# Last expert's second layer and its combination split by 256 columns, layer-norm sums taken in halves, and uneven first input pieces, in a hybrid encoder layer

## The chip, the cores and the metric

The kernel runs on one core of one Trainium2 chip. Its time is the device time of one execution, in microseconds (us). Three runs of the kernel before gave 1277.27, 1277.75 and 1278.08 us, median 1277.75. TensorE (PE) does the matrix products, VectorE (DVE) and ScalarE (ACT) the elementwise work; SyncE (SP) and ScalarE issue the transfers (DMA) discussed here.

## The reference

One layer of a streaming encoder over 256 tokens of width 1024, in float32: a combined input projection, four sequence mixers (gated recurrence, latent attention, a diagonal state-space model, a gated linear recurrence), a gated merge, a layer norm, and then a mixture of experts with a second layer norm. Cut to what this change touches:

```python
proj = x @ w_in                                # first: x and the first 256 columns of w_in
...
top_val, top_idx = lax.top_k(logits, TOP_K)    # 4 of 32 experts a token
top_w = jax.nn.softmax(top_val, axis=-1)
...
y = clamped_swiglu(xb @ w1[e] + b1[e]) @ w2[e] + b2[e]   # each expert, its tokens
out = zeros(n, d).at[slot_token].add(y * slot_w[:, None])
...
x = layer_norm(ALPHA * h + out, ln2_w, ln2_b)  # mean, variance, scale, shift over 1024
```

## The kernel before

Every weight is read once from device memory, 459 MB in all, nearly all of it the experts' (4 MB for w1 and w2 units of 2 MB each, six units an expert). SP issues the weight transfers in one fixed order, each as soon as the place that it writes is free (the semaphore `expert_chunk_used` counts units that PE has used). PE takes them in the same order. Every wait and every order is written out by hand, engine by engine; nothing is scheduled by a planner.

**The start.** PE first multiplies a matrix of ones by itself, eight times (`warm_up(8)`, L937). The activations `xT` (8 rows of 128 x 256, 1 MB) come by ACT's queue and the first chunk of `w_in` (the same size) by SP's, each in four pieces of two eighths; both queues add to the semaphore `first_in[i]` of piece i. PE waits for piece i and does its eight products (L947), 32 instructions of the trace in all, since each float32 product shows as two. Behind the pieces SP issues seven whole chunks of 1 MB at once (rows of 8 KB a partition, where the pieces have 2 KB). ACT issues the small transfer `vec` when piece 2 has landed and the next ones when the last piece has (L582 to L589).

**The end.** The last two experts, 30 and 31, use 64 rows each (CAP, the tokens given to one expert in the main pass). Expert 31's w2 comes as four transfers of 1 MB (L522): first 512 output columns (dh = 0) of both halves of the hidden width, then the others. `last_columns` (L1407) multiplies 64 rows by 512 columns. Its products for even and odd k go to the two halves of the array's columns, so that two run side by side, and the result lies in rows 0 to 63 and 64 to 127 of bank dh as two partial sums. ACT copies each bank (`last_out`, L844). `first_combine` (L1428) multiplies expert 30's result by the token weights, 64 rows deep, and leaves the sum open; `last_combine` (L1436) adds expert 31's, 128 rows deep, since the weights are there twice and so add the partial sums. DVE then adds each of the four 128 x 512 results to `y_acc` and takes the row sum in the same instruction (L2270), and does the layer norm: centre and scale by `ln2_w` (L2277), reciprocal root (L2279), scale and shift by `ln2_b` (L2282), for tokens 0 to 127 (half 0) and then 128 to 255 (half 1). ACT takes the sums of squares between (L869 to L871). SP sends half 0 out whole (L536) and half 1 in two pieces (L539). `ln2_w` and `ln2_b`, 512 KB each as broadcast to 128 partitions, are issued behind the w2 pieces (L524, L525). If an expert has more than 64 tokens, a loop after the main pass does the rest; in the profiled execution DVE passes it by (L2238).

## Time and profile before

| what | value |
|---|---|
| median of three runs | 1277.75 us |
| the profiled execution | 1277.71 us |
| its span (first to last instruction) | 1275.9 us |
| mean granted TensorE clock | 0.996 |
| PE busy | 1236.8 us, 97% |
| DVE / ACT busy | 457.0 / 219.1 us |
| transfers | 458.63 MB, mean 359 GB/s |

The execution is 1.81 us longer than its span, which lies outside what the trace shows. From about 415 us on, the slices of the profile show 414 to 435 GB/s until the end; before that the rate is mostly 127 to 270. PE's busy time counts matmuls that wait in the pipeline, so 97% does not mean that it could do no more.

### The profile page before, as it was taken

What the parts mean: (1) busy time and instruction counts of PE and PEld (TensorE: products, weight loads), DVE (VectorE), ACT (ScalarE), POOL (GpSimd) and SP (SyncE); (2) the same over time, 40 slices, a digit from 0 to 9 for tenths busy, and PEclk for the clock granted to TensorE, in tenths of its full rate; (3) what the DMA queues carried; (4) which work ended last, traced back from release to release, by engine and by line L of the source; (5) the groups of instructions that cost most, each with busy time, mean ns of one, the idle gap of its engine ahead of it and who ended that gap; (6) DMA issues with size and microseconds to landing.
All of it is one profiled execution on the core that took longest, in us unless ns stands there. A gap on an engine that the chain in (4) does not pass through costs nothing.

```text
span 1275.9 us, 14764 instructions
## 1 busy us (share of the span) xinstructions
PE 1236.8 (97%) x6060; PEld 635.1 (50%) x6060; DVE 457.0 (36%) x915; ACT 219.1 (17%) x428; POOL 2.9 (0%) x14
## 2 busy tenths in 40 slices
PE   9999999999999999999999999999999999899996
PEld 8888888888863343333433333333323333333432
DVE  5999926636344512122121213212121313122123
ACT  1722124230041110101101011110101010110102
POOL 0000000000000000000000000000000000000000
PEclk9999999999999999999999999999999999999998
DMA  9533334346979999999999999999999999999996
GB/s 379 206 133 137 127 134 168 127 165 244 423 269 414 428 433 425 429 432 432 431 432 432 429 435 429 434 430 432 430 432 432 431 433 428 431 430 427 426 425 259
DMA packets 31486, 458.63 MB, mean 359 GB/s; under 512 B 4913, under 2 KB 5169, under 8 KB 9426
## 3 DMA queue, kind: packets, MB, share of 16 engines
q1 hardware_dynamic: 27728, 453.00, 84.5%
q10 hardware_dynamic: 3714, 5.00, 1.2%
q8 instruction: 33, 0.54, 0.2%
q14 instruction: 11, 0.09, 0.0%
HBM read 456.94 MB, written 1.05 MB: 359 GB/s over the span
## 4 chain that ended last, share of the span: by engine, by line
PE 73%; DMA 16%; DVE 7%; issue 1%; ACT 1%; DVEq 0%; SPq 0%; POOL 0%; POOLq 0%
PE banks L1345 20%; DMA store<-in_moe_w 16%; PE banks L916 15%; PE banks L1381 14%; PE banks L1353 4%; PE banks L930 4%; PE banks L1172 2%; PE banks L1197 2%; DVE store L2136 2%; PE banks L1452 2%; PE banks L1261 2%; PE banks L1363 1%; DVE store L2133 1%; DVE store L2135 1%; DVE store L2130 1%
## 5 line engine op out<-in xcount | busy, mean ns | idle before, releaser
L1345 PE MATMUL banks<-store 128*64 128x512 f32 x1536 | 344.0, 597 | 15.6 <-DMA store<-in_moe_w 15.3
L1345 PEld LDWEIGHTS banks<-store 128*64 128x64 f32 x1536 | 109.3, 137 | 232.2 <-issue 208.0
L1381 PE MATMUL banks<-store 128*64 128x512 f32 x952 | 210.8, 595 | 0.0
L916 PE MATMUL banks<-store 128*128 128x256 f32 x896 | 197.0, 380 | 0.0
L916 PEld LDWEIGHTS banks<-store 128*128 128x128 f32 x896 | 169.3, 190 | 26.4 <-issue 3.8
L2130 DVE TENSOR_SCALAR store<-banks 128x512 f32<-128x512 f32 x32 | 22.1, 692 | 429.3 <-PE banks L1353 429.3
L1381 PEld LDWEIGHTS banks<-store 128*64 128x64 f32 x952 | 65.8, 137 | 142.8 <-issue 120.1
L1353 PE MATMUL banks<-store 128*64 128x512 f32 x512 | 116.8, 598 | 0.4 <-DMA store<-in_moe_w 0.4
L2144 DVE COPY store<-banks 64x512 f32<-64x512 f32 x30 | 20.8, 694 | 202.9 <-PE banks L1381 202.9
L795 ACT ACTIVATE store<-store 128x512 f32<-128x512 f32 x28 | 17.6, 630 | 431.3 <-DVE store L2130 431.3
L1353 PEld LDWEIGHTS banks<-store 128*64 128x64 f32 x512 | 34.3, 136 | 70.1 <-issue 67.7
L1261 PEld LDWEIGHTS banks<-store 128*128 128x128 f32 x480 | 56.9, 191 | 23.5 <-issue 23.5
L1261 PE MATMUL banks<-store 128*128 128x128 f32 x480 | 63.7, 281 | 0.0
L1452 PE MATMUL banks<-store 128*128 128x512 f32 x120 | 63.5, 631 | 0.0
L930 PE MATMUL banks<-store 128*128 128x256 f32 x256 | 56.2, 379 | 0.1
L930 PEld LDWEIGHTS banks<-store 128*128 128x128 f32 x256 | 48.3, 190 | 7.3 <-issue 1.0
L784 ACT ACTIVATE store<-banks,ln_cols 128x128 f32<-128x128 f32 x128 | 46.4, 475 | 3.1 <-PE banks L1261 1.9
L803 ACT ACTIVATE store<-banks 64x512 f32<-64x512 f32 x28 | 16.5, 589 | 169.5 <-PE banks L1381 169.5
L1452 PEld LDWEIGHTS banks<-store 128*128 128x128 f32 x120 | 19.1, 188 | 43.7 <-issue 43.7
L2154 DVE TENSOR_TENSOR store<-store,banks 128x512 f32<-128x512 f32 x60 | 37.4, 681 | 1.0 <-PE banks L1472 0.9
L1197 PE MATMUL banks<-store 32*64 32x512 f32 x256 | 34.8, 613 | 0.0
L2136 DVE SCALAR_TENSOR_TENSOR store<-store 128x512 f32<-128x512 f32 x32 | 33.6, 1050 | 1.1
(386 smaller groups left out, 827.1 us busy)
## 6 DMA issues: line engine op xcount, KB each, us to landing
store<-in_moe_w SPq DMA_DIRECT2D x72, 4096.0 KB, 30.3
store<-in_moe_w SPq DMA_DIRECT2D x36, 2048.0 KB, 15.1
store<-in_w_in SPq DMA_DIRECT2D x30, 1024.0 KB, 4.9
store<-in_moe_w SPq DMA_DIRECT2D x18, 1024.0 KB, 9.2
store<-in_w_branch SPq DMA_DIRECT2D x8, 1024.0 KB, 4.9
store<-in_w_out SPq DMA_DIRECT2D x4, 1024.0 KB, 6.7
store<-in_w_last SPq DMA_DIRECT2D x4, 1024.0 KB, 34.8
store<-in_w_first SPq DMA_DIRECT2D x4, 256.0 KB, 4.3
```

The source lines that it names most:

```text
L784: ins = nc.scalar.activation(xg[:, k, :], src, ACT.Identity, scale=ln1_cols[:, 2 * KD + k:2 * KD + k + 1], bias=ln1_cols[:, 3 * KD + k:3 * ...
L916: last = mm(b[:, j * SEQ:(j + 1) * SEQ], w[:, k, j * P:j * P + P], xT[:, k, :], start=k == 0, stop=k == KD - 1)
L930: last = mm(bank[3 + u % 2][:, i * SEQ:(i + 1) * SEQ], w[:, k, c * P:(c + 1) * P], yT[:, br, k, :], start=k == 0, stop=k == 3)
L1197: mm(bank[into[i]][64 * ct:64 * ct + 64, :], esel[r:r + NE, :], b1_all[r:r + NE, :], start=True, stop=False, tile_position=(r, 64 * ct))
L1261: last = mm(bank[2 + k // 4][:, (k % 4) * P:(k % 4) * P + cols], h_tok[:, half, k * P:k * P + P], sel[:, half, 0:cols], start=half == 0, s ...
L1345: last = mm(bank[into[i]][64 * ct:64 * ct + 64, :], xg[:, 2 * c + kk, col:col + CAP], w[:, kk, i * FF + ct * 512:i * FF + ct * 512 + 512], ...
L1353: last = mm(bank[into[i]][64 * ct:64 * ct + 64, :], xg[:, 2 * c + kk, col:col + CAP], w[:, kk, i * FF + ct * 512:i * FF + ct * 512 + 512], ...
L1381: last = mm(bank[4][64 * dh:64 * dh + 64, :], actT[:, j, 64 * fh:64 * fh + 64], w[j][:, 512 * dh:512 * dh + 512], start=(fh, j) == (0, 0), ...
L1452: mm(bank[COMB_BANK[i]][:, :], wselT[0:rows_, half, :], y_pair[0:rows_, 512 * dh:512 * dh + 512], start=True, stop=True).then_inc(S["comb_ ...
L2130: V.tensor_scalar(g1, bank[from_[0]][:, :], LIMIT, None, ALU.min).then_inc(S["gmin_ready"], 1)
L2136: V.scalar_tensor_tensor(g1.rearrange("p (j q) -> p q j", j=4), g2.rearrange("p (q j) -> p q j", j=4), 1.0, g3.rearrange("p (q j) -> p q j ...
L2154: ins = V.tensor_tensor(dst, dst, bank[COMB_BANK[i]][:, :], ALU.add)
```

## The change

Five things change.

1. The input pieces are one, two, two and three eighths. The first chunk and `xT` are stored so that each piece is contiguous in device memory. The warm-up has six products.
2. Expert 31's w2 is laid out by quarters of columns: a transfer holds columns 256 i to 256 i + 255 of both 512-column groups. `last_columns` multiplies by 256 columns and puts the two groups (dh) on the two halves of the array's columns, with one full sum each and no partial ones. The last 1 MB is two transfers of 512 KB, the first of which uses `first_in[0]` again, and SP waits for it before it issues `ln2_w` and `ln2_b`.
3. ACT's copies are 128 x 256. `last_combine` is 64 rows deep, eight products of 256 columns, and writes other places (`LAST_BANK`) than `first_combine`, which is now closed by itself.
4. DVE adds expert 30's four results by themselves (four TENSOR_TENSOR), before the test for the extra loop. PE's last combination waits for these.
5. DVE's four sums with a row sum are now half 0 (i = 0, 1), then half 1. The wait for `ln2_in` comes behind them. Then both L2277 instructions, and after them the scale, shift and output of half 0 and half 1.

```diff
+LAST_BANK = ((6, 2), (4, 0))
+FIRST_ROWS = ((0, 1), (1, 3), (3, 5), (5, KD))
...
             for i in range(pieces):
-                ks = slice(KD // pieces * i, KD // pieces * (i + 1))
-                sp.dma_start(first[:, ks, :], src[i]).then_inc(first_in[i], 16)
+                ks = FIRST[i]
+                src = A["w_first"][0, P * CW * ks.start:P * CW * ks.stop].rearrange("(p k n) -> p k n", p=P, n=CW)
+                sp.dma_start(first[:, ks, :], src).then_inc(first_in[i], 16)
...
-            for dh in range(2):
+            for i in range(2):
                 for c in range(NW1, NU):
-                    sp.dma_start(tail_at(NE - 1, c)[:, SLOT * dh:SLOT * dh + SLOT], A["w2_last"][c - NW1, dh]).then_inc(late_landed[late(NE - 1, c, dh)], 16)
+                    if (i, c) == (1, NU - 1):
+                        for part, signal in ((slice(0, D), first_in[0]), (slice(D, SLOT), late_landed[late(NE - 1, c, i)])):
+                            sp.dma_start(tail_at(NE - 1, c)[:, SLOT:][:, part], A["w2_last"][c - NW1, i][:, part]).then_inc(signal, 16)
+                    else:
+                        sp.dma_start(tail_at(NE - 1, c)[:, SLOT * i:SLOT * i + SLOT], A["w2_last"][c - NW1, i]).then_inc(late_landed[late(NE - 1, c, i)], 16)
             sp.wait_ge(S["expert_chunk_used"], LAST - 3)
+            sp.wait_ge(first_in[0], 48)
...
-            warm_up(8)
+            warm_up(6)
...
-                for k in range(4):
-                    r = 64 * (k % 2)
-                    last = mm(bank[dh][r:r + 64, :], actT_last[:, k, 64 * fh:64 * fh + 64], w[:, k, :],
-                              start=(fh, k // 2) == (0, 0), stop=(fh, k // 2) == (1, 1))
+                for k in range(4):
...
+                    for dh in range(2):
+                        last = mm(bank[i][64 * dh:64 * dh + 64, 0:CW], actT_last[:, k, 64 * fh:64 * fh + 64], w[:, k, CW * dh:CW * dh + CW],
+                                  start=(fh, k) == (0, 0), stop=(fh, k) == (1, 3))
...
-            def last_combine(dh):
-
-                pe.wait_ge(S["ypair_lo"] if dh == 0 else S["ypair_hi"], NE)
+            def last_combine(i):
+
+                pe.wait_ge(S["ypair_hi"] if i else S["ypair_lo"], NE)
+                pe.wait_ge(S["comb_used"], NPAIR * 4 + 4)
                 for half in range(2):
-                    mm(bank[COMB_BANK[2 * half + dh]][:, :], wselT_last[1][:, half, :], y_columns[dh], start=False, stop=True).then_inc(S["comb_psum"], 1)
+                    for dh in range(2):
+                        r = 64 * dh
+                        last = mm(bank[LAST_BANK[i][half] + dh][:, 0:CW], wselT_last[1][r:r + 64, half, :], y_last[1][r:r + 64, CW * i:CW * i + CW],
+                                  start=True, stop=True, tile_position=(r, 0))
+                    last.then_inc(S["comb_psum"], 1)
...
+            for half in range(2):
+                for i in range(2):
+                    piece, added = last_pieces(i, half)
+                    dve.wait_ge(S["comb_psum"], (NPAIR + 1) * 4 + 2 * i + half + 1)
+                    ins = V.scalar_tensor_tensor(piece, added, 1.0, piece, ALU.mult, ALU.add,
+                                                 accum_out=small[:, 316 + 2 * half + i:317 + 2 * half + i])
+                link(ins)
...
             dve.wait_ge(S["ln2_in"], 32)
...
```

PE at the start of the program, before. Line 937 is the warm-up, 947 the first chunk, each row a run of equal products:

```order
L937 MATMUL banks<-ones 128x128 [waits ones_ready]
L937 MATMUL banks<-ones 128x128 x7
L947 MATMUL banks<-store 128x256 [waits first_in0]
L947 MATMUL banks<-store 128x256 x3
L947 MATMUL banks<-store 128x256 [waits first_in1]
...
L947 MATMUL banks<-store 128x256 [waits first_in3]
L947 MATMUL banks<-store 128x256 x3
```

PE at the same place after the change (lines 944 and 954 are the same two):

```order
L944 MATMUL banks<-ones 128x128 [waits ones_ready]
L944 MATMUL banks<-ones 128x128 x5
L954 MATMUL banks<-store 128x256 [waits first_in0]
L954 MATMUL banks<-store 128x256
L954 MATMUL banks<-store 128x256 [waits first_in1]
...
L954 MATMUL banks<-store 128x256 [waits first_in3]
L954 MATMUL banks<-store 128x256 x5
```

Two products of the first piece have gone to the last, and two warm-up products are gone.

DVE at the end, before. 2270 adds and sums, 2277 centres, 2279 is the reciprocal, 2282 scales and shifts:

```order
L2264 MEMSET small 128x1 [waits ln2_in]
L2270 SCALAR_TENSOR_TENSOR store,small<-banks,store 128x512 [waits comb_psum,f_chain] x3
L2273 TENSOR_SCALAR small<-small 128x1 [waits f_chain]
L2270 SCALAR_TENSOR_TENSOR store,small<-banks,store 128x512 [waits comb_psum]
L2273 TENSOR_SCALAR small<-small 128x1 [waits f_chain]
L2277 SCALAR_TENSOR_TENSOR store<-store,small 128x1024 [waits sum_ready]
L2279 RECIPROCAL small<-small 128x1 [waits rs_ready,f_chain]
L2282 SCALAR_TENSOR_TENSOR store<-store,small 128x1024 [waits f_chain]
L2277 SCALAR_TENSOR_TENSOR store<-store,small 128x1024 [waits sum_ready]
```

DVE there after the change (2294, 2302, 2306 and 2309 are these four):

```order
L2288 MEMSET small 128x1
L2294 SCALAR_TENSOR_TENSOR store,small<-banks,store 128x2x256 [waits comb_psum,f_chain]
L2294 SCALAR_TENSOR_TENSOR store,small<-banks,store 128x2x256 [waits comb_psum]
L2297 TENSOR_SCALAR small<-small 128x1 [waits f_chain]
L2294 SCALAR_TENSOR_TENSOR store,small<-banks,store 128x2x256 [waits comb_psum] x2
L2297 TENSOR_SCALAR small<-small 128x1 [waits f_chain]
L2302 SCALAR_TENSOR_TENSOR store<-store,small 128x1024 [waits sum_ready,ln2_in]
L2302 SCALAR_TENSOR_TENSOR store<-store,small 128x1024
L2306 RECIPROCAL small<-small 128x1 [waits rs_ready,f_chain]
L2309 SCALAR_TENSOR_TENSOR store<-store,small 128x1024 [waits f_chain]
```

The second centring instruction has moved ahead of the first half's last one, and the wait for `ln2_in` behind the sums.

## Rows read from the trace of the kernel before

**Rows 1.** The page's chain of work that ended last, by engine.

```profile
PE 73%; DMA 16%; DVE 7%; issue 1%; ACT 1%; DVEq 0%; SPq 0%; POOL 0%; POOLq 0%
```

**Rows 2.** Timeline, 0 to 30 us: start, length, engine, line, operation, count, idle before.

```profile
0.79 1.86 ACTq L581 DMA_DIRECT2D store<-in_xT  x4
1.04 3.78 PE L937 MATMUL banks<-ones 128*128 128x128 f32 x16 [1.04 <-POOL ones L551]
4.62 7.78 PE L947 MATMUL banks<-store 128*128 128x256 f32 x32
9.92 0.33 ACTq L586 DMA_DIRECT2D spare<-in_lru_wa  x1
```

**Rows 3.** Issue to landing: all in_w_first; all in_xT; in_xT's second and third.

```profile
DMA to landing us min/median/max: 3.0/4.3/5.9
DMA to landing us min/median/max: 3.3/4.9/7.7
DMA to landing us min/median/max: 4.2/4.9/5.5
```

**Rows 4.** Durations on line 947; then the chain's row of line 916 behind it.

```profile
L947 PE MATMUL banks<-store x32: 379/379/634, 4.6 to 12.0; 128*128 128x256 f32 x32
...
12.40 20.72 PE banks L916 x96
```

**Rows 5.** Queue rows of windows 5:6 us, 9:10 us, and 1252:1253 us.

```profile
q1 hardware_dynamic: 109, 0.20, 53.2%
q10 hardware_dynamic: 99, 0.20, 52.0%
...
q1 hardware_dynamic: 51, 0.37, 91.8%
q10 hardware_dynamic: 43, 0.02, 8.0%
...
q1 hardware_dynamic: 62, 0.43, 104.3%
```

**Rows 6.** Timeline, 1235 us to the end.

```profile
1255.80 1.99 PE L1433 MATMUL banks<-store 64*128 64x512 f32 x8
1257.73 5.48 PE L1414 MATMUL banks<-store 128*64 128x512 f32 x24
1263.14 3.70 PE L1440 MATMUL banks<-store 128*128 128x512 f32 x8
1263.25 0.60 ACT L847 ACTIVATE store<-banks 128x512 f32<-128x512 f32 x1 [2.95 <-PE banks L1414]
1266.95 0.68 DVE L2270 SCALAR_TENSOR_TENSOR store<-banks,store 128x512 f32<-128x512 f32 x1
1267.81 1.28 DVE L2277 SCALAR_TENSOR_TENSOR store<-store,small 128x1024 f32<-128x1024 f32 x1
1269.32 1.28 DVE L2282 SCALAR_TENSOR_TENSOR store<-store,small 128x1024 f32<-128x1024 f32 x1
1270.63 0.34 SPq L536 DMA_DIRECT2D out<-store  x1
1272.03 1.41 DVE L2282 SCALAR_TENSOR_TENSOR store<-store,small 128x512 f32<-128x512 f32 x2
1272.81 1.00 SPq L539 DMA_DIRECT2D out<-store  x2
```

**Rows 7.** The chain of waits, 30 to 420 us: four narrow products side by side.

```profile
179.94 1.86 PE banks L912 x32
```

**Rows 8.** Issue to landing: the four in_w_last (issued from 1216.7); the last in_ln_b.

```profile
DMA to landing us min/median/max: 32.0/34.8/37.1
DMA to landing us min/median/max: 30.5/30.5/30.5
```

**Rows 9.** DMA issues, 1225 to 1276 us: size and median to landing.

```profile
out<-store SPq DMA_DIRECT2D x1, 512.0 KB, 2.6
out<-store SPq DMA_DIRECT2D x2, 256.0 KB, 2.0
```

More of the change, by code:

```diff
@@ L288, in encoder_layer @@
         assert [slot_of[("wo", i)] for i in range(4)] == [4, 5, 6, 7]
-        pieces = 4
+        FIRST = [slice(*rows) for rows in FIRST_ROWS]
+        pieces = len(FIRST)
         first_in = [sem(f"first_in{i}") for i in range(pieces)]
@@ L576, in link @@
                 act.wait_ge(S["a_chain"], ac[0])
-            x_rows = A["xT"].rearrange("i p (k t) -> i p k t", k=KD // pieces)
             for i in range(pieces):
-                ks = slice(KD // pieces * i, KD // pieces * (i + 1))
-                act.dma_start(xT[:, ks, :], x_rows[i]).then_inc(first_in[i], 16)
+                ks = FIRST[i]
+                x_rows = A["xT"][0, P * SEQ * ks.start:P * SEQ * ks.stop].rearrange("(p k t) -> p k t", p=P, t=SEQ)
+                act.dma_start(xT[:, ks, :], x_rows).then_inc(first_in[i], 16)
             act.wait_ge(first_in[pieces // 2 - 1], 32)
@@ L842, in _, with last_out @@
             expert(NE - 3, 1, NPAIR - 2, NPAIR - 1)
-            def last_out(dh):
-                act.wait_ge(S["expert_chunk_used"], LAST + 5 + dh)
-                nc.scalar.activation(y_columns[dh], bank[dh][:, :], ACT.Copy).then_inc(S["ypair_hi"] if dh else S["ypair_lo"], 1)
+            def last_out(i):
+                act.wait_ge(S["expert_chunk_used"], LAST + 5 + i)
+                nc.scalar.activation(y_last[1][:, CW * i:CW * i + CW], bank[i][:, 0:CW], ACT.Copy).then_inc(S["ypair_hi"] if i else S["ypair_lo"], 1)
             sigmoid(NE - 2)
@@ L945, in _ @@
                 for j in range(2):
-                    for k in range(KD // pieces * i, KD // pieces * (i + 1)):
+                    for k in range(FIRST[i].start, FIRST[i].stop):
                         last = mm(bank[2 * j][:, 0:SEQ], w[:, k, j * P:j * P + P], xT[:, k, :], start=k == 0, stop=k == KD - 1)
@@ L1552, in _ @@
                     second_layer(item_unit(j), j + NE)
-                    combine(j + NPAIR, j + NE + 1, CAP, range(4), j * 4 + (NPAIR + 1) * 4)
+                    combine(j + NPAIR, j + NE + 1, CAP, range(4), j * 4 + (NPAIR + 2) * 4)
         @block.vector
@@ L2234, in _, with last_pieces @@
             V.tensor_copy(y_last[0][64:128, :], bank[4][64:128, :]).then_inc(S["ypair_hi"], 1)
-            dve.wait_ge(S["comb_used"], NPAIR * 4)
+            def last_pieces(i, half):
+                return (y_acc[:, half, :].rearrange("p (d n) -> p d n", d=2)[:, :, CW * i:CW * i + CW],
+                        banks[:, LAST_BANK[i][half]:LAST_BANK[i][half] + 2, 0:CW])
+            for dh in range(2):
+                for half in range(2):
+                    dst = y_acc[:, half, 512 * dh:512 * dh + 512]
+                    dve.wait_ge(S["comb_psum"], NPAIR * 4 + 2 * dh + half + 1)
+                    V.tensor_tensor(dst, dst, bank[COMB_BANK[2 * half + dh]][:, :], ALU.add).then_inc(S["comb_used"], 1)
+            dve.wait_ge(S["comb_used"], (NPAIR + 1) * 4)
             n_items = dve.value_load(item_e[0:1, NITEM:NITEM + 1], min_val=0, max_val=NITEM)
@@ L2238, in _ @@
             with dve.If(n_items > 0):
-                dve.wait_ge(S["comb_psum"], (NPAIR + 1) * 4)
-                for i in range(4):
-                    half, dh = i // 2, i % 2
-                    dst = y_acc[:, half, 512 * dh:512 * dh + 512]
-                    V.tensor_tensor(dst, dst, bank[COMB_BANK[i]][:, :], ALU.add).then_inc(S["comb_used"], 1)
-                dve.wait_ge(S["comb_used"], (NPAIR + 1) * 4)
+                dve.wait_ge(S["comb_psum"], (NPAIR + 2) * 4)
+                for i in range(2):
+                    for half in range(2):
+                        dst, added = last_pieces(i, half)
+                        V.tensor_tensor(dst, dst, added, ALU.add).then_inc(S["comb_used"], 1)
+                dve.wait_ge(S["comb_used"], (NPAIR + 2) * 4)
                 V.memset(small[:, 509:510], 0.0).then_inc(S["spilled"], 1)
@@ L2251, in _ @@
                     second_out(j + NE, 0)
-                    dve.wait_ge(S["comb_used"], j * 4 + (NPAIR + 1) * 4)
-                    combine(j + NPAIR + 1)
                     dve.wait_ge(S["comb_used"], j * 4 + (NPAIR + 2) * 4)
-                for i in range(4):
-                    ins = V.memset(bank[COMB_BANK[i]][:, :], 0.0)
+                    combine(j + NPAIR + 2)
+                    dve.wait_ge(S["comb_used"], j * 4 + (NPAIR + 3) * 4)
+                for i in range(8):
+                    ins = V.memset(bank[i][:, 0:CW], 0.0)
                 ins.then_inc(S["spilled"], 1)
```

42 lines of the change are left out of this document (20 added, 22 removed).

## The prediction

> **What bounds the kernel now.** I read the chain of waits first. It lies on PE for 73% and on DMA for 16% of the span [rows 1]. Behind the first chunk it stays on PE [rows 4], and its DMA pieces come only late in the experts, where each transfer was released by what PE had used. So a microsecond at the start counts in full. Between start and end the change alters nothing. So two stretches are read in the timeline: the first 12 us and the last 25 us.
>
> At the start, the warm-up runs without a gap into the first chunk, whose first product starts at 4.62 us [rows 2]. Products of one form take up to 634 ns there and 379 later [rows 4]: TensorE first works at the lower of its two levels (1.2 GHz, then 2.4), although the windows of the profile print a granted clock of 1.00 for it. A product record of 256 columns takes 20.72/96 = 0.216 us at the higher level [rows 4]. The 32 records from 4.62 to the next chunk's first product at about 12.23 us take 7.61 us, 0.70 more than 32 x 0.216 = 6.91. At half speed a record would take 0.43, so 0.70/0.216 is some 3.3 records, up to about 6.0 us. ACT issues its next transfer at 9.92 us [rows 2], when `xT`'s last piece has landed (issued at 2.2, 7.7 us to landing [rows 3]). PE reaches that piece at 12.23 - 8 x 0.216 = 10.50 us: 0.6 us of slack, no wait.
>
> At the end, w2's four pieces land at 1253.8 (1216.7 + 37.1) and then 2.5 us apart, the last at 1261.2 (issued 1229.2, 32.0 to landing [rows 8]). PE takes 1.72 us for each, has the combination of expert 30 between (1.99), and ends them at 1263.1. Then come 3.70 us of combination, and DVE's fourth sum starts at 1266.95, right behind the last product [rows 6]. From L2277 at 1267.81 on DVE is a chain of its own to 1273.44, and the last output piece (issued 1273.47, 2.0 us to landing [rows 9]) sets the end.
>
> **The start, step by step.** Two warm-up products less are 4 records of 0.213 us (3.78 for 16, less the last one's pipeline, [rows 2]): 0.85 us. PE can start real work at 3.77. But this is time at the lower level: 0.85 us there are 0.43 us at the higher. With no new wait the next chunk starts at 12.23 - 0.43 = 11.80. The first piece is half as large. The old one, 512 KB, landed at 4.1 (0.79 + 3.3 [rows 3]), so I put the new one at about 3.5, in time. Piece 2 ends at three eighths, between the old landings at 4.1 and 5.45 (1.25 + 4.2): 4.8, and PE wants it 4 slow records later, at 5.5. Piece 3 lands between 5.45 and 7.25, wanted at 7.5. Piece 4 is wanted at 11.80 - 12 x 0.216 = 9.2. All 2 MB are needed for it, as for the old one, which landed at 9.9. **Here is a new wait.** From a landing L the next chunk starts at L + 0.05 + 2.59.
>
> - L stays at 9.9: 12.54 instead of 12.23, a loss of 0.3.
> - Break-even is L = 9.6.
> - L at or before 9.2: the gain of 0.43.
>
> What sets L? `xT`'s last piece lands 1.8 us behind the chunk's (8.1 = 2.2 + 5.9). An 8 KB row occupies one of the 16 engines 0.315 us (104.3% of 16 us over 53 such rows; the nine others of 62 are semaphore writes), a 2 KB row 0.084 (52.0% of 16 us over 99) [rows 5]. At 9 to 10 us the two queues move 51 large and 43 small rows [rows 5], nearly one for one. So an engine that has finished its share of the chunk gives `xT` one 2 KB row for each 8 KB row of the following chunks, 0.40 us a turn, and 1.8 us are 4.5 turns. In the change the rows are 1, 2, 2 and 3 KB, eight to an engine and piece as before, and 3 KB should take about 0.125. If `xT` lags by as many rows, 4.5 turns of 0.44 are 2.0 us, while the chunk's end comes 0.2 earlier since more of `xT` is still to come: L = 9.9. If it lags by as many bytes, 3 turns: 9.4. If the lag is a late start of ACT's queue of some 0.4 us, it is 5 rows of 2 KB but 9 of 1 KB, nobody catches up in a one-for-one game, and working the turns through gives 1.0 us more: L = 10.9. I take 9.9, the middle one and the row itself, and keep 9.2 (-0.43) and 10.9 (12.23 becomes 13.54, +1.3).
>
> The Trainium skill, DMA: Bandwidth & Descriptors, section Queues, rings and completion order, says that an engine goes round its queues by packets of several descriptors, not by single ones. By that a piece's eight rows leave in one turn, whatever their size, the last piece of `xT` stands behind the chunk's last and one turn of 8 KB rows, and L stays at 9.9: the sum would be the same +0.3, and the 10.9 would fall away. The counts at 9 to 10 us are means over 16 engines and don't decide it.
>
> The chunk behind is not wanted before 11.8, and its bytes stand right behind these. ACT's `vec` is issued earlier, with piece 2, but stands behind the same bytes as now. If the chunk came late too, its wait would add to this term.
>
> **The end, step by step.** `last_columns` has twice the products of half the columns, in pairs: 8 pair records of 0.216 are 1.73 for a piece, as now. The row for four narrow products of 256 columns side by side gives 1.86/8 = 0.23 [rows 7]: at worst 0.13 a piece, 0.5 in four. I take nothing, since wide and narrow rows agree within the pipeline's last drain. The last 1 MB in two: PE reaches it at 1261.21, its first half has landed near 1260.0, the second (1261.2) is wanted 0.86 later; the restart of 0.1 goes. PE is through at 1263.0.
>
> `last_combine`: 8 pair records of 0.216 instead of 8 of 0.43, so 2.0 us with the drain instead of 3.70 (L1433, the same depth, took 1.99 for the same number of columns). Its wait for expert 30's additions: four of DVE at 0.68 [rows 6] from about 1257.0, done by 1259.8 beside PE's products. The scalar load and branch behind them have 4 us, until 1263.8. ACT's second copy has half the columns, 0.4 of 0.60, hidden behind i = 0.
>
> DVE: the first sum can start at 1263.8, the second (third result) at 1264.65, half 1's two follow at 0.69 each: end 1266.9, row sum and mean to 1267.24. So L2277 starts at 1267.24 instead of 1267.81, 0.57 earlier. `ln2` is issued when the first half of the last 1 MB has landed, 1260.0, starts 0.7 later (as L536's store does), and has 256 rows of 4 KB, 16 an engine at 0.16 (half an 8 KB row) = 2.6 us: landed at about 1264.5. Even at twice that it is there at 1267.1. An L2277 and the reciprocal behind it take 1269.32 - 1267.81 = 1.51, and an instruction of 1024 columns with another behind it 1272.03 - 1269.32 - 1.51 = 1.20 [rows 6]. So half 0's L2282 starts at 1267.24 + 1.20 + 1.51 = 1269.95 and ends near 1271.24, **0.64 later** than now (1270.60), since half 1's centring stands before it; half 1's pieces end at 1272.1 and 1272.76, 0.68 earlier than now (1273.44).
>
> But the stores go through one queue. Half 0 now leaves at 1270.63 and is done (2.6 us) before half 1's first piece is issued at 1272.81. Changed, it is issued at 1271.27, moves data from 1272.0 to 1273.4, and the two pieces behind it take about half as long each, 0.75: 1274.9 against 1275.1 now (1.4 us for 512 KB and the 0.7 to its first byte are my split of L536's 2.6, with 0.5 for the landing). Of DVE's 0.68 only 0.2 is left; bounds 0.45 (no gaps between the stores) and -0.3 (if the columns cost their 0.5). I take a gain of 0.25.
>
> **Sum.** +0.3 - 0.25 = +0.05 on the execution's 1277.71, which stands 0.04 below the median: 1277.8 us.
>
> **The rivals.**
>
> - *Everything at the start arrives in time* (L up to 9.4). For it: 3 KB rows hold their own better against 8 KB ones, and the total is the same. Against: the old landing of 9.9 [rows 2, 3]. -0.43 - 0.25: 1277.1.
> - *The input queue falls behind* (slower). `xT`'s first rows of 1 KB are traded against 2 KB ones of the chunk, the last 3 KB ones against 8 KB ones; PE stands at its piece 4 for 1.7 us. It decides from L = 9.8 on, where the loss exceeds the end's gain. For it: `xT` lands 0.3 us behind the chunk at the first piece and 1.8 at the last [rows 3]. Price at L = 10.9: +1.3 - 0.25, 1278.8.
> - *The narrow products cost what L912's do*: the end loses 0.3, with the start 0.3: 1278.4.
> - *The clock rises later.* PE did not stop between 1.04 and the rise near 6 us. With the shorter warm-up a first piece that lands after 3.8 leaves a hole. Each microsecond more at 1.2 GHz costs half of one; if the rise came 3 us later, 1.5: 1279.3. The Trainium skill, TensorE: Matmul & The Clock Gate, section Part 1: The HAM clock gate, has the clock follow recent busyness, not a count of products; by that the shorter warm-up alone costs nothing, and only such a hole would.
>
> **How the numbers follow.** Forecast (both terms small, 1277.4 to 1278.2) 0.41; in time 0.23; input queue behind 0.23; narrow products 0.08; clock 0.05. The likeliest is 1277.8. The range 1276.8 to 1279.0 takes in the start's bounds from -0.43 with the end's best of 0.45 to +1.3. A change of 0.2% is 2.55 us, about what a measurement here can tell from none, and no case reaches it but the clock's worst or an end that I have misread on either side: faster 0.03, same 0.94, slower 0.03.
>
> **What would show it.** Right: the first product of the first chunk at 3.8; a DMA wait of about 0.7 us before its last 12 records; L916 starting near 12.5; ACT's `lru_wa` issued near 9.9; L1453 taking 2.0 us; L2302 at 0.6 us earlier against PE's last column product; the first store 0.6 us later than now and the three back to back. Wrong: `lru_wa` at 10.5 or later (queue behind) or before 9.4; records of 634 ns beyond 6 us; L2302 waiting for `ln2_b`; L1424 over 1.8 us a piece.

## The result, and the profile after

The changed kernel takes 1279.42 us (median of 20 executions, 1278.08 to 1280.55), the kernel before beside it 1277.47 (20, 1276.44 to 1279.65): ratio 1.0014, 95% interval 1.0008 to 1.0020. It is 1.95 us slower where 0.05 was forecast, and 0.4 us above the range of 1276.8 to 1279.0. The profiled execution took 1280.46 (span 1278.7), one of the two slowest of the 20, against 1277.71 and 1275.9 before.

The chain of waits by engine, where DMA had 16% in [rows 1], now has 17%:

```profile
PE 73%; DMA 17%; DVE 7%; ACT 1%; issue 1%; DVEq 0%; ACTq 0%; SPq 0%
```

The timeline of the changed kernel, 0 to 16 us, in the columns of [rows 2]:

```profile
0.79 1.85 ACTq L588 DMA_DIRECT2D store<-in_xT  x4
1.04 2.93 PE L944 MATMUL banks<-ones 128*128 128x128 f32 x12 [1.04 <-POOL ones L558]
3.76 4.21 PE L954 MATMUL banks<-store 128*128 128x256 f32 x12
9.09 1.99 PE L954 MATMUL banks<-store 128*128 128x256 f32 x8 [1.12 <-DMA store<-in_xT]
12.16 0.33 ACTq L593 DMA_DIRECT2D spare<-in_lru_wa  x1
12.19 2.86 PE L954 MATMUL banks<-store 128*128 128x256 f32 x12 [1.10 <-DMA store<-in_xT]
14.88 1.46 PE L923 MATMUL banks<-store 128*128 128x256 f32 x6
```

PE starts at 3.76, 0.86 earlier, as planned. Then it stands twice for `xT` and reaches the next chunk at 14.88 instead of 12.23: 2.65 later. ACT issues `lru_wa` as soon as the last piece has landed, so its start gives the landing: 12.16, against 9.92 in [rows 2]. That is past the 10.5 which the prediction named as the sign of a queue that falls behind. The chain of waits of 0 to 30 us says the same (start, length, what):

```profile
2.19 9.95 DMA store<-in_xT
12.14 0.04 issue
12.19 2.86 PE banks L954 x12
```

Issue to landing, `in_w_first` and then `in_xT`, is to be read beside [rows 3]: the chunk's median and first are quicker, its last is 0.6 slower, and `xT`'s last is 2.3 slower.

```profile
DMA to landing us min/median/max: 2.5/3.9/6.5
DMA to landing us min/median/max: 2.9/5.6/10.0
```

The shift goes through: the router's product in the middle, at 370.87 us, is 2.65 later than before (368.22). The timeline of the end, against [rows 6]:

```profile
1257.02 1.95 PE L1424 MATMUL banks<-store 128*64 128x256 f32 x16 [0.64 <-DMA store<-in_w_last]
...
1260.82 5.40 PE L1424 MATMUL banks<-store 128*64 128x256 f32 x48
...
1263.51 0.43 SPq L532 DMA_DIRECT2D store<-in_ln_b  x1
...
1266.15 2.00 PE L1453 MATMUL banks<-store 64*128 64x256 f32 x16
...
1270.30 2.48 DVE L2302 SCALAR_TENSOR_TENSOR store<-store,small 128x1024 f32<-128x1024 f32 x2
...
1273.01 1.28 DVE L2309 SCALAR_TENSOR_TENSOR store<-store,small 128x1024 f32<-128x1024 f32 x1
...
1274.32 0.34 SPq L543 DMA_DIRECT2D out<-store  x1
...
1275.18 1.00 SPq L546 DMA_DIRECT2D out<-store  x2
```

From the last expert's first column product to the end of the span it is 1278.7 - 1257.02 = 21.68 us; before, 1275.9 - 1253.93 = 21.97: 0.29 gained. The combination takes 2.00 instead of 3.70, DVE's L2302 starts 13.28 behind the first column product instead of 13.88, and no instruction waits for `ln2_b`. The stores come back to back, and the last two now take longer to land than in [rows 9]:

```profile
out<-store SPq DMA_DIRECT2D x1, 512.0 KB, 2.6
out<-store SPq DMA_DIRECT2D x2, 256.0 KB, 2.5
```

So +2.65 at the start, -0.29 at the end, and +0.4 between them, where the change does nothing and two executions of one kernel differ by as much (below): +2.75, which is 1280.46 - 1277.71.

### The profile page after: what moved, and what is told of

It is laid out like the page before. It is cut to its first block, busy times and chain, and to the rows that moved or that the text cites. A ratio compares the mean times of both kernels' runs of the same rounds, so it can differ in the third digit from the quotient of the medians.

```text
span 1278.7 us, 14842 instructions
## 1 busy us (share of the span) xinstructions
PE 1235.7 (97%) x6096; PEld 637.1 (50%) x6096; DVE 459.6 (36%) x919; ACT 218.9 (17%) x428; POOL 2.9 (0%) x14
## 3 DMA queue, kind: packets, MB, share of 16 engines
HBM read 456.94 MB, written 1.05 MB: 358 GB/s over the span
## 4 chain that ended last, share of the span: by engine, by line
PE 73%; DMA 17%; DVE 7%; ACT 1%; issue 1%; DVEq 0%; ACTq 0%; SPq 0%
PE banks L1352 20%; PE banks L923 15%; PE banks L1388 14%; DMA store<-in_moe_w 13%; PE banks L1360 4%; PE banks L937 4%; DMA store<-in_w_last 3%; PE banks L1179 2%; PE banks L1204 2%; DVE store L2151 2%; PE banks L1467 2%; PE banks L1268 2%; PE banks L1370 1%; DVE store L2148 1%; DVE store L2150 1%; DVE store L2145 1%
## 5 line engine op out<-in xcount | busy, mean ns | idle before, releaser
L2145 DVE TENSOR_SCALAR store<-banks 128x512 f32<-128x512 f32 x32 | 22.1, 692 | 429.9 <-PE banks L1360 429.9
```

What stands on the lines that cost most here:

```text
L2145: V.tensor_scalar(g1, bank[from_[0]][:, :], LIMIT, None, ALU.min).then_inc(S["gmin_ready"], 1)
```

## The experiments

Every kernel ran beside the kernel before, whose medians are in the third column. A row is what one DMA engine moves for one partition; each of the 16 engines moves eight rows of a piece. The column "`xT` last landed" has the landing of the input's last piece, with the chunk's in brackets where that came later. "Next chunk" is the start of PE's first product of the following chunk. "The later landing" is the later one of `xT`'s and the first chunk's last pieces. Landings and starts are those of one traced execution each. The letters in the expectations are theories, and each says what it claims there. At the start A means: the loss is in the input pieces, since ACT's queue starts late, an engine serves the two queues row for row, and so its lag is a number of rows, paid in 8 KB rows at the end. (In e1 and e3 it says only that the loss is in the pieces, in e12 it is about the stores.) A kernel with five pieces of 1, 1, 2, 2 and 2 eighths (e10) gave no result.

| kernel | time us | before us | ratio, 95% | `xT` last landed | next chunk |
|---|---|---|---|---|---|
| before | | | | 9.92 | 12.23 |
| the change | 1279.42 | 1277.47 | 1.0014 (1.0008 to 1.0020) | 12.16 | 14.88 |
| e1, end only | 1277.18 | 1277.79 | 0.9995 (0.9986 to 1.0004) | 9.69 | 12.18 |
| e2, pieces only | 1279.84 | 1277.79 | 1.0017 (1.0008 to 1.0026) | 11.37 | 14.09 |
| e3, warm-up only | 1277.83 | 1277.79 | 1.0000 (0.9991 to 1.0009) | 10.22 | 12.07 |
| e4, small rows behind | 1279.22 | 1277.79 | 1.0010 (1.0001 to 1.0019) | 11.02 | 13.81 |
| e5, next chunks held | 1278.81 | 1277.71 | 1.0014 (1.0005 to 1.0023) | 9.93 | 13.90 |
| e6, even, held | 1278.26 | 1277.71 | 1.0005 (0.9996 to 1.0014) | 8.68 | 12.67 |
| e7, 3-2-2-1 | 1278.16 | | one run | 9.07 | 13.04 |
| e8, queues swapped | 1278.31 | | one run | 9.1 (chunk 10.39) | 13.10 |
| e9, no 3 KB rows | 1279.5 | | one run | 11.21 | 13.93 |
| e11, stored apart | 1279.53 | | one run | 11.37 | 14.08 |
| e12, half 0 first | 1277.21 | 1277.67 | 0.9995 (0.9986 to 1.0004) | 9.68 | 12.39 |
| e13, e2 without lead | 1278.90 | 1277.56 | 1.0010 (1.0001 to 1.0019) | 8.3 (chunk 9.2) | 12.6 |
| e14, small first rows | 1278.89 | | one run | 11.6 | 13.49 |
| e15, change without lead | 1279.49 | 1277.56 | 1.0014 (1.0005 to 1.0023) | 9.0 (chunk 9.8) | 13.50 |
| e16, end, even, no lead | 1277.33 | 1277.73 | 0.9996 (0.9986 to 1.0005) | 8.5 (chunk 9.2) | 12.52 |
| e17, even, no lead | 1277.54 | | one run | 8.1 (chunk 9.0) | 12.39 |
| e18, the change again | 1278.78 | | one run | 11.39 | 14.11 |
| e19, e2 again | 1279.16 | | one run | 11.15 | 13.87 |

### The parts by themselves: e1, e2, e3

The change with even pieces and the old warm-up:

```diff
-FIRST_ROWS = ((0, 1), (1, 3), (3, 5), (5, KD))
+FIRST_ROWS = ((0, 2), (2, 4), (4, 6), (6, KD))
-            warm_up(6)
+            warm_up(8)
```

> The changed end with the start as before (four pieces of two eighths, warm-up of eight). Theory A (the loss is the start's input pieces, the end gains): the span from the first column product of the last expert to the end is 21.7 us as in the changed kernel (22.0 before), xT's last piece lands near 9.9 us, the second chunk starts at 12.2 us; time 0.3 us under before. Theory B (the end or the middle costs the time, the start's wait is absorbed later): 1 us or more above before.

The kernel before with the change's pieces (`FIRST_ROWS` and its storage) and nothing else:

> Before, with only the pieces of 1, 2, 2 and 3 eighths; warm-up of eight. Theory A: the small first rows let ACT's queue fall behind, whatever the warm-up is: xT's last piece lands at 11 to 12.2 us, the second chunk starts at 13.7 to 14.9, the time is 1.5 to 2.7 us above before. Theory C (the shorter warm-up is what costs, by a hole in PE's work and a clock that rises later): the second chunk starts at 12.2 to 12.6, the time is that of before within 0.4 us.

The kernel before with `warm_up(6)`:

> Before, with only the warm-up cut from eight products to six. Theory A: harmless; xT's last piece lands near 9.9, wanted at 10.1, the second chunk starts at 11.8 to 12.0, time 0.2 to 0.4 us under before. Theory C: products of 634 ns beyond 6.1 us, the second chunk later than 12.2, time above before.

The loss is in the pieces: e2 has all of it (2.05 us), e1 and e3 have none. The end alone takes 21.7 us from the first column product (before 21.97), as in the change; its 0.6 us below the kernel before is not told from zero. The warm-up alone moves nothing, where 0.2 to 0.4 us less was expected: PE waits 0.37 us for the first piece and 0.27 for the last.

### What stands behind: e4, e5, e6

e4 is the change with the second and third chunk in 2 KB rows instead of 8 KB:

```diff
-                sp.dma_start(slot(slot_of[c], *shape), src).then_inc(landed[i % R1], 16)
+                if i in (1, 2):
+                    for ks in (slice(k, k + 2) for k in range(0, KD, 2)):
+                        sp.dma_start(slot(slot_of[c], *shape)[:, ks], src[:, ks]).then_inc(landed[i % R1], 16)
```

> The changed kernel, with the second and third chunks of w_in (the transfers queued right behind the first chunk on SP's queue) each moved in four transfers with rows of 2 KB a partition instead of one with 8 KB. Theory A (an engine gives the two queues a row each in turn, so xT's lagging rows of 3 KB are each held up by an 8 KB row): the turn is 0.21 instead of 0.44 us, so xT's last piece lands about 9 turns x 0.23 = 2 us earlier, near 10 us, and the second chunk starts near 12.7 (14.9 in the changed kernel); time about 2 us under the changed kernel. Theory D (turns of several rows, or a slow engine whatever is queued beside): the last piece lands at 11.5 or later.

`xT` lands at 11.02, between the two theories: A had asked for 10, D for 11.5 or more. e5 is the change with the second chunk held until the third piece is in; e6 is the same with even pieces:

```diff
+                if i == 1:
+                    sp.wait_ge(first_in[2], 32)
```

> The changed kernel, and SP waits for the third input piece (first_in[2] at 32) before it issues the second chunk of w_in and all behind it, so that no 8 KB row is in the queues beside xT's last piece, or for at most its last microsecond. Theory A (8 KB rows, one for each row of xT, hold its last piece up): it lands 2 us or more earlier than the changed kernel's 12.2, near 9 to 9.5 us, and the second chunk starts at 12 to 12.3; time 1279.4 less some 2.5 us, under before by 0.3. The rate of 250 to 330 GB/s between 4 and 7 us that all runs with uneven pieces show stays, if it is the pieces' own. Theory D (one slow engine, whatever is beside it): the last piece lands at 11 or later.

> The changed end, warm-up of six, even pieces (two eighths each), and SP's wait for the third piece before the next chunks. Theory A: xT's last piece lands at 8 to 8.5 us instead of 9.7 to 10.2, PE has no wait there (wanted at 10.1), the second chunk starts at 11.8 to 12.0 if it has landed by then; with the end's 0.6 the time is 0.8 us under before. Rival: the second chunk, issued at 7.3 instead of 2.6, lands after 11.8 and PE waits for it, and the time is that of the changed end alone (1277.2).

The timeline of e5:

```profile
8.74 4.98 SPq L437 DMA_DIRECT2D store<-in_w_in  x8
8.77 4.58 PE L956 MATMUL banks<-store 128*128 128x256 f32 x20 [1.25 <-DMA store<-in_xT]
9.93 0.34 ACTq L595 DMA_DIRECT2D spare<-in_lru_wa  x1
...
13.90 2.40 PE L925 MATMUL banks<-store 128*128 128x256 f32 x10 [0.54 <-DMA store<-in_w_in]
```

Without 8 KB rows beside it `xT`'s last piece is in at 9.93, 2.2 sooner than in the change's first trace and 1.5 sooner than in its second (e18, below). So the 8 KB rows cost the last piece most of its delay. They are not the whole of it: the third piece landed at 8.73, nearly as late as in the change (9.04), and SP issued the first 8 KB row only then. A had asked for 9 to 9.5 and for a next chunk at 12 to 12.3. The time is not won: PE stands 1.25 us for the third piece, and the held chunk is now late itself (0.54).

In e6 `xT` is in at 8.68, and still the next chunk starts at 12.67 instead of near 11.8. The chunk isn't late there, though its last signal came at 12.27, so that 11.8 could not have been reached. PE began its first product at 4.26 instead of 3.76, since it waited for the first piece, and the clock rose late, at 7.13 us. The products' durations from 5.7 us on (0.63 us at 1.2 GHz, 0.38 at 2.4), first e6 and then e3, with the same warm-up:

```profile
L956 PE MATMUL banks<-store x4: 454/631/631, 5.7 to 7.0; 128*128 128x256 f32 x4
```

```profile
L947 PE MATMUL banks<-store x6: 379/379/379, 5.7 to 6.8; 128*128 128x256 f32 x6
```

Single DMA rows show more than a landing does. These are the starts (us) of the last 3 KB rows of `xT` on all 16 engines, from the trace's DMA records:

```
the change, first trace   9.07  9.14  9.19  9.62 10.04 10.46 10.89 11.31
the change, second trace  9.64  9.74 10.01 10.02 10.16 10.59
e13 (lead removed)        7.72  7.75  7.80  7.89  7.99
```

In the first trace all engines but one have started their last row by 9.2. The last one hands out five more rows 0.42 to 0.43 us apart: one 8 KB row (0.31) and one of 3 KB (0.12) by turns. This straggler alone sets the landing: of the 32 signals that the two last pieces give, 16 each, 31 are in at 9.82 and the last at 12.14 (before: 9.18 and 9.90). In the second trace four are in after 10.4, and in e19 the last two at 11.05 and 11.13, so there it is several engines. The straggler was late before the 8 KB rows: its signal for the third piece came at 9.04, all others by 7.89. The Trainium skill, DMA: Bandwidth & Descriptors, section Queues, rings and completion order, has an engine drain a packet of several descriptors from one queue before it turns to the other. This trace disagrees, with 0.42 us from row to row on the straggler; by the rule, as the prediction applied it, the eight rows would have left in one turn, and the landing would have stayed near 9.9.

### Other shapes and places: e7, e8, e9, e11, e14

e7 is e2 with pieces of 3, 2, 2 and 1 eighths; e8 the change with `xT` on SP and the chunk on ACT; e9 the change with the last piece as a 1 KB and a 2 KB transfer; e11 is e2 with the pieces stored at steps of 256 KB; e14 the kernel before with only its first pieces cut in two:

```diff
e7:  +FIRST_ROWS = ((0, 3), (3, 5), (5, 7), (7, KD))
e8:  -                sp.dma_start(first[:, ks, :], src).then_inc(first_in[i], 16)
     +                act.dma_start(first[:, ks, :], src).then_inc(first_in[i], 16)
e9:  +for part in ((slice(0, 1), slice(1, 3)) if i == 3 else (slice(0, ks.stop - ks.start),)):
e11: +A["xT"][0, P * SEQ * 2 * i:P * SEQ * (2 * i + ks.stop - ks.start)]
e14: +for part in ((slice(0, 1), slice(1, 2)) if i == 0 else (slice(0, 2),)):
```

> Before, with pieces of 3, 2, 2 and 1 eighths, warm-up of eight. Theory A (a queue that starts 0.4 us late lags by that many rows, and big first rows make it few): xT lags the chunk by at most 1.3 us at the last piece, which lands at 9.3 or before. Its first piece lands near 4.8, and PE stands still for 0.4 us before it. Rate between 4 and 7 us: 390 GB/s if only small first rows lower it, 250 to 330 if any uneven pieces do.

> The changed kernel with xT's pieces issued by SP and the chunk's by ACT. Theory A (it is ACT's queue that lags, whatever it carries): xT lands near 8.7 us and the first chunk's last piece at 11 to 12.2; time as the changed kernel's. Rival E (it is xT's place in memory or its destination that is slow): xT still lands last, at 11 to 12.

> The changed kernel, with the last input piece of both queues moved as two transfers (rows of 1 KB, then of 2 KB), so that no row of 3 KB exists. Theory F (3 KB rows slow the engines between 4 and 7 us): 390 GB/s there, and xT's third piece lands near 7.5 instead of 9.05. Theory A alone (small first rows make ACT's queue lag in rows, and the lag stays): the rate stays at 300 to 330, the third piece at 8.5 to 9.

> The kernel before with pieces of 1, 2, 2 and 3 eighths and warm-up of eight (as in the run with the pieces only), but each piece stored at a multiple of 256 KB in device memory, as the even pieces were. Theory G (the rate drop between 4 and 7 us comes from where the two streams read in device memory): 390 GB/s there, xT's third piece near 7 (8.1 without), its last at 10.5 or earlier (11.4 without). If the placement has no part: the rate 250 to 330 GB/s and the landings as without.

> Before (even pieces, warm-up of eight), with the first piece of each queue moved as two transfers with rows of 1 KB. Theory A: the lead of 0.4 us is up to nine rows instead of five; xT's last piece lands at 10.7 to 11.5 instead of 9.9. Rival I (the size of the last rows sets it, the first ones have no part): 9.7 to 10.2.

Issue to landing in e8, first `in_xT` (SP), then `in_w_first` (ACT):

```profile
DMA to landing us min/median/max: 2.3/4.2/6.9
DMA to landing us min/median/max: 2.7/5.0/8.2
```

The lag belongs to ACT's queue, whatever it carries, but it is 1.3 us here instead of 3.5, and the chunk's last piece lands at 10.39 where A had asked for 11 to 12.2. The 3 KB rows are not needed for the late landing (e9: 11.21), nor does the place in memory take it away (e11: 11.37). Small first rows are enough: e14 keeps 2 KB rows everywhere but in the first 512 KB, and `xT` lands at 11.6 instead of 9.9. (Its queues have one transfer more, but so have e9's, which land no later than e2's.) With large first rows (e7) it lands at 9.07, and PE waits 0.47 us early on. Each of these five is a single execution.

### The lead of SP's queue: e13, e15, e17, e16

The lead is the earlier start of SP's queue. Both queues get their first issue at 0.79 us, yet in the 16 traces of kernels that leave this order alone the first row on SP's queue starts at 1.79 to 2.23 (in all but two by 1.82) and the first on ACT's at 1.97 to 2.56, 0.17 to 0.76 behind SP's. e13 (e2), e15 (the change) and e17 (the kernel before) let SP wait until POOL's second memset is done, so that its first issue comes 0.36 us later; e16 is e1 with this and `warm_up(6)`:

```diff
+            sp.wait_ge(S["g_chain"], 1)
             shape, _ = chunk_source(STREAM[0])
```

> Before with the pieces of 1, 2, 2 and 3 eighths and warm-up of eight (the run with the pieces only), and SP waits for GpSimd's second memset (done at 1.1 us) before its first transfer, so that its queue no longer starts 0.4 us ahead of ACT's. Theory A (the lead at the start, counted in small rows, is what ACT's queue never makes good): xT's last piece lands within 1 us of the chunk's, at 8.5 to 9.5 instead of 11.4, the second chunk starts at 12.0 to 12.3 and the time is before's within 0.5 us. Rival H (the small first rows slow the transfers themselves between 4 and 7 us, the lead has no part): xT's last piece lands at 11 or later again, time 1.5 to 2 us above before.

> The changed kernel, with SP's first transfer behind GpSimd's second memset as in the run without the lead. Theory A: xT's last piece lands at 9 to 9.5, PE waits for it by at most 0.3 us, the second chunk starts at 11.8 to 12.2, time 1277.0 (1279.4 for the changed kernel). Rival H: the time of the changed kernel.

> The kernel before with the chunk's transfers on SP issued 0.36 us later, all else as it was. A (late start of ACT's queue): the input's last piece lands near 8.3, the chunk's near 9.2; the later of the two comes 0.6 to 0.7 before the old 9.9. H (small rows): the input's last piece stays at 9.9 and the chunk's at 8.1 or a little later. The next chunk starts at 12.2 in both, since TensorE wants the last piece at 10.5 only.

> The change's end, even pieces at the start (2 rows of 256 columns each, 2 KB), warm-up of 6, and the chunk's transfers on SP issued 0.36 us later, so that ACT's queue starts first. If the lag of the input's queue comes from its late start (A), the input's last piece lands near 8.3 and the chunk's near 9.3 instead of 9.9 for the later of the two; TensorE wants it at 9.2, so the next chunk starts at 11.8 to 11.95 (before: 12.23) and the time is 0.3 to 0.4 under the end's alone: 0.7 to 0.9 under before. If small first rows alone cause the lag (H), nothing changes with even pieces: the later of the two lands at 9.9, the next chunk starts at 12.5, and the time is 0.2 over the end's alone, 0.2 to 0.4 under before.

The queue row of 1.5 to 2 us (packets, MB, busy), in the change (SP's is q1) and in e13 (ACT's is q10); the other queue has no row yet in either:

```profile
q1 hardware_dynamic: 23, 0.02, 35.2%
```

```profile
q10 hardware_dynamic: 42, 0.04, 33.1%
```

The timeline of e17, where nothing else differs from [rows 2], and its landings, `in_w_first` and then `in_xT`:

```profile
0.79 1.84 ACTq L582 DMA_DIRECT2D store<-in_xT  x4
...
1.15 1.82 SPq L424 DMA_DIRECT2D store<-in_w_first  x4
...
9.04 0.34 ACTq L587 DMA_DIRECT2D spare<-in_lru_wa  x1
```

```profile
DMA to landing us min/median/max: 3.0/5.7/6.5
DMA to landing us min/median/max: 2.7/4.4/5.9
```

The wait of 0.36 us turns the order of the queues round in all four. `xT` lands at 8.1 instead of 9.9 with even pieces, at 8.3 instead of 11.4 in e13, at 9.0 instead of 12.2 in e15. The later landing is 9.0 to 9.9, now the chunk's, and the next chunk comes 1.5 us (e13) and 1.4 us (e15) sooner. So in these traces the queue that starts first is the one that ends first. That the lag is a count of rows is not shown, and three things speak against it:

- The late start does not go with the late landing. ACT's first row came 0.21 us behind SP's in the change (landing 12.16), 0.19 in e2 (11.37), 0.43 in the kernel before (9.92) and 0.75 in e1 (9.69).
- In the mean over the engines `xT` was not further behind. When SP's queue started the chunk's last row, 20 (the change), 36 (its second trace), 46 (e2) and 51 (e19) of `xT`'s 512 rows had not started; with even pieces it was 38 (before), 60 (e1) and 62 (e3).
- In the first trace one engine in sixteen was late, where a late start of the queue alone should hold back all of them.

The medians give back less: e13 stands 1.34 us above the kernel before beside it, where e2 stood 2.05 above; e15 stands 1.93 above, the change 1.95. So in e15, expected at 1277.0, an earlier landing in the trace goes with no gain in the median at all. Start and end of their traces explain only +0.4 (e13) and 1.27 - 0.3 = +1.0 (e15). e13's trace is of the second fastest of its 11 executions, e15's of the fourth fastest. The timelines of e15 and then of e16 show where the rest can go:

```profile
7.35 6.31 PE L955 MATMUL banks<-store 128*128 128x256 f32 x28 [1.68 <-DMA store<-in_w_first]
```

```profile
7.24 5.45 PE L955 MATMUL banks<-store 128*128 128x256 f32 x24 [0.58 <-DMA store<-in_w_first]
```

Here the chunk's second piece is the late one (7.3 and 7.2). In e16 the next chunk starts at 12.52 instead of the 11.8 that A gave, and the kernel is no better than e1. How this piece lands in other executions no trace shows, so this stays a guess for the medians.

### The spread: e18, e19

e18 is the change and e19 is e2, each traced a second time.

> The changed kernel once more, for a second trace: its first was one of the two slowest of 20 executions (1280.46 against a median of 1279.42). If the landing of the input's last piece at 12.16 is what the change always does, it lands within 0.3 of it again and the time lies by other things; if the landing itself varies from one execution to the next, a time near 1279.2 goes with a landing near 11.

> The pieces alone once more, for a second trace: the input's last piece landed at 11.37 in the first. Again within 0.3 of it, if the landing belongs to the pieces; up to 0.8 away, if it varies from one execution to the next and the 12.16 of the whole change and these 11.37 are two draws of the same.

The second timeline of the change:

```profile
7.76 2.00 PE L954 MATMUL banks<-store 128*128 128x256 f32 x8 [0.36 <-DMA store<-in_xT]
...
11.39 0.33 ACTq L593 DMA_DIRECT2D spare<-in_lru_wa  x1
11.41 2.86 PE L954 MATMUL banks<-store 128*128 128x256 f32 x12 [1.66 <-DMA store<-in_xT]
...
14.11 2.11 PE L923 MATMUL banks<-store 128*128 128x256 f32 x9
```

The landing varies (12.16 and 11.39; e2 11.37 and 11.15); in all four it is 1.2 to 2.3 us later than the 9.92 before. From the next chunk to the first column product it is 1242.14 and 1241.14 us in the two traces, 1241.70 before: the middle varies by 0.5 either way. A part of this can be TensorE's clock. The window 1014 to 1016 us, clock third from the right, in the first trace and in the second:

```profile
1014.00:1016.00 2.00, 2.00 (x8) 0.73 (x6) 0.32 (x2) 0.00 (x0) 0.00 (x0) 0.50 1.01 426
```

```profile
1014.00:1016.00 2.00, 2.00 (x12) 0.72 (x10) 0.00 (x0) 0.00 (x0) 0.00 (x0) 1.00 1.14 492
```

Such a stretch at 1.2 GHz, 3.4 us long (6.8 in e2's first trace), begins between 1009 and 1014 us in ten of the 20 traces, the kernel before's among them. It belongs to no kernel: of the change's two traces and of e2's two, one has it and one has not. The two traces stand 2.75 and 1.07 above the kernel before; the medians differ by 1.95, about their mean.

### The order at the end: e12

e1 with DVE finishing half 0 before it centres half 1:

```diff
             for half in range(2):
-                ins = V.scalar_tensor_tensor(h_tok[:, half, :], ...)
-            link(ins)
-            for half in range(2):
+                link(V.scalar_tensor_tensor(h_tok[:, half, :], ...))
                 dve.wait_ge(S["rs_ready"], 6 + half)
```

> The changed end with the start as before, and DVE finishes half 0 (centre, reciprocal, scale and shift) before it centres half 1, as the kernel before did. Theory A (the changed order lets half 0's store leave 0.64 us later, and the three stores behind each other give back 0.4 us of DVE's gain): DVE's end is at most 0.1 us later, the first store leaves 1.2 us earlier, and the span from the last expert's first column product to the end is 21.3 us instead of 21.7; time 0.3 us below the changed end's 1277.2. Rival (the stores are not what sets the end): 21.7 to 21.8.

```profile
1262.09 1.08 PE L1424 MATMUL banks<-store 128*64 128x256 f32 x8 [0.44 <-DMA store<-in_w_last]
1263.10 2.00 PE L1453 MATMUL banks<-store 64*128 64x256 f32 x16
...
1270.08 0.34 SPq L543 DMA_DIRECT2D out<-store  x1
...
1272.26 1.00 SPq L546 DMA_DIRECT2D out<-store  x2
```

The first store leaves 6.98 us behind L1453 instead of 8.17 in e1, and the end of the span comes 12.30 behind it instead of 12.57: 1.2 us earlier for half 0 are worth 0.27, since the last piece still ends the chain. A late last transfer in this execution (PE waits 0.44) puts L1453 0.66 us later behind the first column product than in e1. So the end takes 22.1 us in all instead of the 21.3 expected, and the median is that of e1.

## Why the prediction was wrong

- **The term that failed** is the start, and in it the sentence "I take 9.9, the middle one and the row itself". The landing L was 12.16 (11.39 in the second trace). The formula behind it held: L + 0.05 + 2.59 gives 14.80, measured 14.88. The term is +2.65 (+1.88) instead of +0.3. e2 shows it by itself, with 2.05 us on the median.
- **Why L was so late.** The prediction counted rows in the mean over 16 engines. The mean did not get worse than with even pieces, as the counts above show; single engines did, up to one that started its last row 2.1 us after all others. With small first rows some rows of 1 to 3 KB take up to 19 times their usual time, which no term had (last section); whether they are what makes an engine late stays open. e5 shows that the 8 KB rows make an engine's lateness dear.
- **The outcome was the rival** "the input queue falls behind", given 0.23, and its sign, `lru_wa` after 10.5, came. Its working holds only in part. That ACT's queue is the late one, and that the 8 KB rows are the price, e8, e13, e17 and e5 bear out. That the lag is nine rows instead of five no run shows, and the row counts speak against it. Its L = 10.9 was too small, and it does not follow from its own figures either: nine turns of 0.44 us are 4.0 us, which behind a chunk that ends near 7.4 (earlier than 8.1, since nine rows of `xT` an engine are still to come) gives about 11.4, an estimate from the prediction's rows. The 9.4 for "as many bytes" should by the same sum be 9.2.
- **The rule of the Trainium skill** (DMA: Bandwidth & Descriptors, Queues, rings and completion order), by which the 10.9 would fall away, would have kept L at 9.9. The measured turns of single rows on the straggler disagree with it.
- **Pieces 2 and 3** were put at 4.8 and before 7.5. `xT`'s came at 5.05 and 9.04, and PE lost 1.12 us of idle time there, all of it covered by the later wait.
- **"The clock rises later"** (0.05) did not decide: it rose at 6.6 us in the change's trace and at 6.05 before, and the wait for `xT` behind it covers that. In e6 it did cost.
- **The end was right** in the trace: -0.29 against -0.25. No median tells it from zero (e1). L1453 took 2.00 (2.0), L1424 1.95 for the first piece and 5.40 for three (1.94 and 5.48 before, so no cost of narrow products), L2302 came 0.60 earlier (0.57), the first store late and all three back to back, `ln2_b` waited for by nobody. e12 shows the step of the stores by itself, in one trace.

What stays open: what makes single rows slow and single engines late; why ACT's queue starts 0.2 to 0.8 us behind SP's; and the 0.9 us between what the traces explain and the medians in e13 and e15.

## What to carry to other kernels

Before a buffer's pieces are made smaller, look at the last landing on the slowest engine, not at a mean over 16: a piece is in when its last engine is, and one late engine pays for each of its rows with the largest row of the other queue. Where two queues fill one need and one of them starts late, let the other wait: with even pieces this brought the later landing from 9.9 to 9.0 us, and no cost showed, in one execution (e17). By itself that wins nothing, since PE was not waiting, and with uneven pieces it won little or nothing in the median (e13, e15). A piece made smaller to start earlier helps only if every later one is still in time.

## What the runs showed that was not expected

With small first rows the rate is lower for microseconds after they are through. Windows of 1 us from 4 and 5 us (PE, PEld, DVE, ACT, POOL, clock, DMA share, GB/s), before and then e2:

```profile
4.00:5.00 1.00, 1.00 (x5) 0.95 (x5) 0.00 (x0) 0.00 (x0) 0.00 (x0) 1.00 1.04 399
5.00:6.00 1.00, 1.00 (x4) 0.78 (x3) 0.00 (x0) 0.00 (x0) 0.00 (x0) 1.00 1.05 395
```

```profile
4.00:5.00 1.00, 1.00 (x8) 0.92 (x8) 0.00 (x0) 0.00 (x0) 0.00 (x0) 1.00 1.15 248
5.00:6.00 1.00, 1.00 (x6) 0.90 (x5) 0.00 (x0) 0.00 (x0) 0.00 (x0) 1.00 0.81 250
```

With nearly as much busy time (0.98 in the mean against 1.05) the engines move 0.63 of the bytes. The dip is in the change and in every other kernel with small first rows but one (211 to 305 GB/s in the worst window from 4 to 7 us), not in e1 and e3. The one is e11, with its pieces at 256 KB steps: it kept 329 to 372 and landed no sooner, so the dip is not the cause of the lag. But e16 and e17, with even pieces and the lead removed, fell to 250 and 315 from 5 to 6 us: small rows are not its only cause, which was not found.

The DMA records show what the engines do in it: they are busy with rows that take far too long. A row of 2 KB usually takes 0.084 us. Of the rows of 1 to 3 KB that start between 3 and 7 us, none takes 0.2 us before; in the change two rows of 2 KB, at 4.55 and 4.66 us, take 1.53 and 1.57. Every kernel with small first rows has four to 16 such rows of over 0.4 us, e11 too; the kernels with even pieces of 2 KB rows, and e7, have two at most. Whether these rows make the late engine is not shown: e8 has 16 of them, five over 0.9 us at about 4.5 us, and its last two signals are only 0.1 us apart.

TensorE's clock rose between 3.94 us (e13) and 7.13 us (e6) from the start of the span, by the trace's clock records; in the kernel before it was 6.05. It is not a matter of the kernel alone: in the two traces of e2's kernel it rose at 3.96 and 6.75. In e6 the product records start 0.43 us apart before the rise and 0.22 after it, so each microsecond of delay costs half a microsecond wherever PE is the bound.
